# Seven-product down projection of one layer: where the weight combinations are formed, how the products are summed, and which engine norms the rows

## The reference

```python
def conv_ffn(h, rows, cols, w_up, w_dw, b_dw, w_down):
    up = h @ w_up                                   # 1024 -> 2 * 2816
    a, g = jnp.split(up, 2, axis=-1)
    ...                                             # 3x3 depthwise conv of g on the 16 x 64 grid
    g = g4.reshape(B, L, D_FF) + b_dw
    return (jax.nn.gelu(g) * a) @ w_down            # 2816 -> 1024

    ...
    x = layer_norm(ALPHA * x + g2[:, None, :] * ffn, p['ln2_g'], p['ln2_b'])
```

## Time and profile before

| | |
|---|---|
| runs | 1420.64, 1414.67, 1416.58 us; median 1416.58 |
| profiled execution | 1413.91 us, of which the span 1412.2 us |
| mean granted clock | 0.963 |
| PE busy | 1285.5 us (91%), 7739 matmuls |
| DVE busy | 1043.7 us (74%) |
| POOL busy | 636.2 us (45%) |
| ACT busy | 593.4 us (42%) |

### The profile page before, as it was taken

How to read it: one execution, slowest core, us unless ns; L and a number is a source line. 1 busy time by engine, 2 the same in 40 slices (tenths; PEclk the granted TensorE clock), 3 DMA queues, 4 the chain that set the end, 5 groups by cost and what they waited for, 6 DMA issues and landing times.

```text
span 1412.2 us, 21496 instructions
## 1 busy us (share of the span) xinstructions
PE 1285.5 (91%) x7739; PEld 1182.6 (84%) x7739; DVE 1043.7 (74%) x1563; ACT 593.4 (42%) x1018; POOL 636.2 (45%) x453
## 2 busy tenths in 40 slices
PE   5899999889998799988999999999999999999763
PEld 3689998788988677888999999999999878888642
DVE  7565669673566788879786777767656797887997
ACT  6533124435345734544344444444434543443321
POOL 1002998323343112349557666676656640001552
PEclk9899899999999899998999999999999999999886
DMA  9432231553425432202222231322312777654221
GB/s 345 130 88 83 64 90 45 172 174 75 110 75 194 164 113 98 75 16 69 72 92 93 69 108 55 107 87 74 97 51 67 260 268 244 209 192 172 90 74 60
DMA packets 145666, 166.69 MB, mean 118 GB/s; under 512 B 9303, under 2 KB 101939, under 8 KB 145331
## 3 DMA queue, kind: packets, MB, share of 16 engines
q1 hardware_dynamic: 145102, 160.88, 35.5%
q0 software_dynamic: 288, 4.72, 0.8%
q10 hardware_dynamic: 197, 0.06, 0.0%
HBM read 137.83 MB, written 27.80 MB: 117 GB/s over the span
## 4 chain that ended last, share of the span: by engine, by line
PE 70%; DVE 15%; issue 4%; ACT 4%; DMA 3%; POOL 3%; SPq 0%; DVEq 0%; ACTq 0%; POOLq 0%
PE ps L1149 12%; PE ps L1495 10%; PE ps L1493 10%; PE ps L1494 10%; PE ps L1525 4%; PE ps L1526 4%; PE ps L1527 4%; PE ps L1101 2%; DVE dwlo L3018 1%; DMA adaw<-in_w_ada 1%; PE ps L1060 1%; PE ps L1369 1%; PE ps L1371 1%; PE ps L1370 1%; DVE qk L2612 1%
## 5 line engine op out<-in xcount | busy, mean ns | idle before, releaser
L2924 DVE SCALAR_TENSOR_TENSOR ps<-gs,taps,ps 128x945 f32<-128x945 f32 (+2 forms) x176 | 215.8, 1226 | 36.2 <-ACT ps L1910 30.8
L1525 PE MATMUL ps<-dwhi,uhi 128*128 128x512 f32 x341 | 137.9, 404 | 26.5 <-DVE dwlo L3018 22.2
L1149 PE MATMUL ps<-h1hi,whi 128*128 128x384 f32 x432 | 155.1, 359 | 0.0
L1149 PE MATMUL ps<-h1lo,whi 128*128 128x384 f32 x432 | 147.6, 342 | 0.0
L1149 PE MATMUL ps<-h1hi,wlo 128*128 128x384 f32 x432 | 147.4, 341 | 0.0
L1526 PE MATMUL ps<-dwlo,uhi 128*128 128x512 f32 x341 | 136.3, 400 | 0.0
L1527 PE MATMUL ps<-dwhi,ulo 128*128 128x512 f32 x341 | 136.0, 399 | 0.0
L1525 PEld LDWEIGHTS ps<-dwhi,uhi 128*128 128x128 f32 x341 | 65.8, 193 | 46.3 <-issue 18.8
L2109 POOL TENSOR_TENSOR wlo<-raw,whi 128x512 fp32r<-128x512 f32 x46 | 68.9, 1500 | 71.9 <-ACT whi L1605 28.6
L1493 PE MATMUL ps<-thi,xhi 128*128 128x288 f32 x320 | 95.5, 299 | 3.0 <-issue 3.0
L1493 PE MATMUL ps<-thi,whi 128*128 128x288 f32 x320 | 94.2, 294 | 2.1 <-POOL wlo L2109 2.1
(11 more groups left out here) (422 smaller groups left out, 3891.6 us busy)
## 6 DMA issues: line engine op xcount, KB each, us to landing
raw<-in_w_up SPq DMA_DIRECT2D x78, 256.0 KB, 3.4
u_rows<-ub SPq DMA_DIRECT2D x22, 576.0 KB, 2.9
adaw<-in_w_ada SPq DMA_DIRECT2D x24, 512.0 KB, 3.9
raw<-in_w_in SPq DMA_DIRECT2D x40, 256.0 KB, 4.1
w_raw<-in_w_down SPq DMA_DIRECT2D x33, 256.0 KB, 5.1
adaw<-in_w_ada SPq DMA_DIRECT2D x8, 1024.0 KB, 10.6
u_raw<-u_rows SPq DMA_DIRECT2D x22, 320.0 KB, 5.9
raw<-u_rows SPq DMA_DIRECT2D x25, 256.0 KB, 5.3
```

Source lines behind the costliest of these rows:

```text
L1149: last = mm(ps[:, bank, 0:GN], a[:, n % 2, k * P:(k + 1) * P], b[:, kk, grp(g)], start=(kk == 0 and a is whi and b is h1hi), stop=(kk == K ...
L1525: mm(out, u_hi, w_hi, start=start, stop=False)
L2924: step(stt(a3[:, ro, co], g3[:, ri, ci], taps[:, tap:tap + 1], a3[:, ro, co], ALU.mult, ALU.add), 2 + m)
```

## The change

- **Weight combinations in the up projection.** The `t1` to `t4` of the down projection are gone. A new helper `t_parts` on DVE forms all four combinations of one step from the four blocks of w_down in a buffer `st`, with a wait between them, in the up projection: behind `ada3` in every second tile of the first four bodies (8 times) and in the first three tiles of the last body. SP loads `st` (two loads of 512 KB) and stores it to a new array `t_rows` in memory (1 MB) each time. In the down projection every product's weights are loaded through the ring `w_raw`.
- **`ub` is gone.** Its place holds `st`; u is written in place over `val` and stored from there, so ACT's copy of product 1 into `val` also waits for that store.
- **Order and chaining.** The products run D_U1, D_U2, D_S2, D_S1, D_S4, D_S3, D_U4, with a fixed set of banks each (SET). D_S2 is summed on top of D_U1 in PSUM (two of its tiles are written back to PSUM by ACT, `seed`), D_S4 on top of D_S1, D_S3 on top of D_U1 + D_S2, and D_U4 on top of that. ACT copies the intermediate sums out between products (`copy_u2`, `copy_at_end`).
- **Context rows** are done in D_U1 and D_U2 with six matmuls a step each, and no more in D_S4. Their weights' low parts in D_U2 (`xw_lo`) are POOL's, 11 instructions.
- **Norm.** `part` on DVE does gate, residual and statistics of half a row tile, `spread` the aggregate, `gain` normalises and applies gain and bias with two 128x1024 scalar_tensor_tensor. POOL only forms the nine 1/sqrt; ACT does nothing of the norm.
- **SP's order** is new in the down projection: the gate and norm rows (2 MB) are loaded behind D_U2's loads, the x rows of five tiles within D_S2, the others within D_U4, the first store within D_S4.

```diff
             def up_loads(b, jj, blk=None):
 ...
+                if blk is None:
+                    store_st(2 * b + jj, F_0 + 2 * b + jj + 1)
+                    if jj < 2:
+                        sp.wait_ge(st_out, SI_0 + 16 * (2 * b + jj + 1))
+                        load_st(2 * b + jj + 1)
+                elif jj % 2 == 0:
+                    store_st(2 * b + jj // 2, 2 * b + (F_0 + jj // 2 + 1))
+                else:
+                    sp.wait_ge(st_out, 32 * b + (SI_0 + 16 * (jj // 2 + 1)))
+                    load_st(2 * b + (jj // 2 + 1))
 ...
                 act.wait_ge(u_ready, j + (N_PLAIN + jj - 1))
+                act.wait_ge(u_out[par], 8 * j + (UO_0 + 16 * (1 + jj // 2)))
                 fn(halves(val[:, par, second]), ps[:, PC:PC + 2, 0:TC], ACT.Copy).then_inc(x5_copied, 1)
 ...
+            def t_parts(b, n):
+
+                def step(ins, m):
+                    ins.then_inc(st_step, 1)
+                    dve.wait_ge(st_step, 6 * b + (SS_0 + 3 * n + m))
+
+                w11, w12, w21, w22 = [st[:, q, :] for q in range(4)]
+                dve.wait_ge(st_in, 64 * b + (SI_0 + 32 * (n + 1)))
+                step(tt(w11, w12, w11, ALU.subtract), 1)
+                step(tt(w12, w22, w12, ALU.subtract), 2)
+                step(tt(w22, w22, w11, ALU.subtract), 3)
+                tt(w21, w21, w22, ALU.subtract).then_inc(t_formed, 1)
 ...
                 conv(j + (N_PLAIN + jj - 1), 1 - par)
                 if blk is not None:
                     ada3(b, jj, blk)
+                if blk is not None and jj % 2 == 0:
+                    t_parts(b, jj // 2)
+                if blk is None and jj < 3:
+                    t_parts(b, jj)
                 dve.wait_ge(pe_unit, s_unit(b, jj, 4) + 1)
 ...
+            def part(i, half):
+                t, slot, cols = TILE_OF[i], (2 * NT + i) % 4, slice(half * UC, (half + 1) * UC)
+                out, gate = z[t][:, cols], grows2[:, who(t), cols]
 ...
+                else:
+                    dve.wait_ge(pe_zt, N_ZT + 8 + i - 4)
+                    link(tt(out, ps[:, BANKS[0][t], :], gate, ALU.mult))
 ...
+                ins = stt(out, zt[(i - 1) % 4 if i else 4][:, cols], ALPHA, out, ALU.mult, ALU.add)
 ...
+                link(v.bn_stats(stats[:, slot, 6 * half:6 * half + 6], out))
 ...
+            def gain(i, halves=1):
 ...
+                    link(stt(out, out, mv[:, slot, 0:1], lnrows2[:, 0, cols], ALU.subtract, ALU.mult))
+                    stt(out, out, rstd[:, slot, :], lnrows2[:, 1, cols], ALU.mult, ALU.add
+                        ).then_inc(z_ready if halves == 1 else zl_ready, 1)
 ...
             for j in range(KF):
                 both_lo(D_S3, j)
                 if 3 <= j < 7:
                     c12(j - 3)
+                if j == 3:
+                    part(1, 1)
+                    spread(1)
                 if j == 4:
+                    part(2, 1)
+                    spread(2)
                 if j == 5:
+                    gain(1)
                 if j == 6:
+                    part(3, 1)
+                    spread(3)
                 if j == 7:
+                    gain(2)
                 if j == 8:
+                    part(4, 1)
+                    spread(4)
                 if j == 9:
+                    gain(3)
             for j in range(KF):
                 both_lo(D_U4, j)
                 if j == 0:
+                    gain(4)
                 if 3 <= j < 7:
+                    c22(j - 3)
+                if 4 <= j < 8:
+                    part(1 + j, 1)
+            part(5, 0)
+            spread(5)
+            part(6, 0)
+            spread(6)
+            gain(5)
+            part(7, 0)
+            spread(7)
+            gain(6)
+            part(8, 0)
+            spread(8)
+            gain(7)
+            gain(8, halves=2)
```

More of the change, by code:

```diff
@@ L499, in layer @@
         BANKS = ((0, 1, 4, 5), (2, 3, 6, 7))
-        D_U1, D_U2, D_S1, D_S2, D_S4, D_S3, D_U4 = range(7)
+        D_U1, D_U2, D_S2, D_S1, D_S4, D_S3, D_U4 = range(7)
+        SET = (0, 1, 0, 1, 1, 0, 0)
         TILE_OF = (LT, 4, 5, 6, 7, 0, 1, 2, 3)
+        T_ROW = {D_S1: 0, D_S3: 1, D_U4: 2, D_S2: 3}
         def s_count(name, j):
-            return F_0 + KF * ("S3", "S1", "S2", "S4").index(name) + j + 1
-        def t_count(name, j):
-            return F_0 + KF * ("T1", "T2", "T4", "T3").index(name) + j + 1
+            return F_0 + {"S3 ahead": j, "S1": KF + 2 * j, "S2": KF + 2 * j + 1, "S4": 3 * KF + j, "S3": 4 * KF + j}[name] + 1
         def ulo_count(m):
@@ L521, in u_index, with v_index, d_index @@
         def u_index(p, j):
-            return KF * {D_U1: 0, D_U2: 1, D_S2: 2, D_S4: 3, D_U4: 4}[p] + j
-        def w_index(p, j):
-            return KF * {D_U1: 0, D_U2: 1, D_S4: 2, D_U4: 3}[p] + (j - 4 if p == D_U4 else j)
+            return KF * {D_U1: 0, D_U2: 1, D_U4: 2}[p] + j
         def x_index(p, j):
-            return KF * {D_U1: 0, D_U2: 1, D_S1: 2, D_S2: 3, D_U4: 4}[p] + (j - 8 if p == D_U4 else j)
-        def d_index(kind, j):
-            return KF * ("u3", "w22", "w22 again").index(kind) + j
+            return KF * {D_U1: 0, D_U2: 1}[p] + j
+        def v_index(p, j):
+            return KF * {D_U2: 0, D_S2: 1, D_S4: 2}[p] + j
+        def d_index(p, j):
+            return KF * {D_U1: 0, D_S4: 1}[p] + j
         def u_landed(p, j):
@@ L859, in load_u @@
-                if p == D_S4:
-                    load_rows(dst[:, UC:UX], KF + j, slice(LAT, T), done)
-                elif p in (D_U1, D_U2):
+                    at((s_formed, s_count("S3 ahead", j + KF - ARING)) if j < ARING else ulo_count(KF * D_U2 + j - ARING))
+                else:
+                    at(ulo_count(KF * D_U2 + j + KF - ARING if j < ARING else KF * D_U4 + j - ARING))
+                if p == D_U4:
+                    load_rows(dst[:, 0:UC], KF + j, slice(0, UC), done)
+                else:
@@ L967, in _ @@
                 sp.wait_ge(u_out[par], UO_0 + 16 * (FT // 2))
+            for b in range(4):
+                sp.wait_ge(y_out[b], 16 * times(b))
             for j in range(KF):
@@ L971, in _ @@
                 load_x(D_U2, j)
[L972 to L989 removed]
+                load_v(D_U2, j)
+            sp.wait_ge(st_out, SI_0 + 16 * KF)
             sp.wait_ge(gate_out, 16)
@@ L1573, in _ @@
             for p in range(7):
-                ctx = p in (D_U1, D_U2, D_S4)
-                order = {D_U2: (2, 3, 0, 1), D_S1: (1, 2, 3, 0), D_S3: (1, 2, 3, 0)}.get(p, (0, 1, 2, 3))
+                ctx = p in (D_U1, D_U2)
+                order = (2, 3, 0, 1) if p in (D_U2, D_S2) else (0, 1, 2, 3)
                 for j in range(KF - N_TAIL if p == D_U4 else KF):
@@ L1583, in _ @@
                         last = tile_mms(p, j, i)
+                        if p in (D_S1, D_S3) and j == KF - 1 and i < H - 1:
+                            last.then_inc(pe_zt, 1)
                     if ctx and j < KF - 1:
@@ L3061, in t3 @@
[L3061 to L3070 removed]
+                tt(su2[j][:, :], v_part(D_S2, j), su2[j][:, :], ALU.subtract).then_inc(s_formed, 1)
```

694 lines of the change are left out of this document (258 added, 436 removed).

## The result

The changed kernel takes 1395.34 us (median of 4 runs, 1393.13 to 1398.87) against 1416.6: a ratio of 0.9849, 95% interval 0.9819 to 0.9879. On the chip of the first experiments it was 0.9876 (0.9854 to 0.9898). The prediction was 1391, with a range of 1375 to 1408. Spans: 1392.8 us against 1412.2.

A forecast was written before the change was run, and what follows sets the result against it. DVE, often standing behind POOL, was taken to hold up PE at the down projection's end. +13.6 (up projection), -3.5 (D_U1), -34.2 (end) gave -24.1 us, span 1388.1, and 1391 us forecast, range 1375 to 1408.

The forecast's parts named there:

- What bounded it: Down projection: some 40 us of PE waiting or at lower clock, 20.7 us DVE tail; DVE largely stands behind POOL.
- D_S3, D_U4 and the tail: End of the down projection: the end comes 81.2 us after D_S4 instead of 115.4, 34.2 us less.
- The stages between at zero: D_U2, D_S2, D_S1, D_S4: DVE's work fits PE's pace, transfers cost zero, upper bound 5 us.
- D_U1: First down-projection product: fewer DVE combinations take 3.5 us off, between 0 and 5.2, giving 46.6 us.
- The up projection: Four combinations in DVE's 3.20 us gap, taking turns with POOL, make PE wait: 1.7 us a tile, 13.6 for eight.
- The rule of the Trainium skill: Shared SBUF port lock: a turn of 2.0 us instead of 1.69, up projection's price 19 us, forecast 5 us later.
- The sum: Whole kernel: +13.6 - 3.5 - 34.2 = -24.1 us, span 1388.1.
- A: Up projection: the combinations are free there, -37.7 us, about 1378; chance 0.17.
- B: Clock and DVE keep the end, D_U2 transfers cost: 4 + 5 + 3 us more, 19 instead of 13.6, about 1405; chance 0.17.
- C: Up projection: each combination loses two turns to POOL, 3.3 us each, +26 us, 1442; chance 0.08.

The follow-up runs named there:

- e5: The kernel before with only gate and bias of the last norm moved from POOL to DVE: 1408.54 us, ratio 0.9936 to before.
- e4: The changed kernel with sixteen extra POOL instructions of 128x1024 on unused memory during the last eight row tiles: 1426.12 us, ratio 1.0056 to before.
- e0: The changed kernel run again without any edit, as yardstick: 1399.05 us, ratio 0.9876 to before.
- e1: The split version: changed kernel with two combinations ahead of the add of product 4, two behind that of product 5: 1381.51 us, 0.9766 of before.
- e6: The changed kernel with all four combinations of a step behind the add of product 5: 1381.52 us, ratio 0.9757 to before.
- e7: The mixed version: changed kernel with all four combinations behind product 5's add in looped bodies, unchanged in the last body: 1380.73 us, 0.9748 of before.
- e2: The changed kernel with combinations on one column instead of 512, loads, stores and waits kept, results wrong: 1383.07 us, ratio 0.9764 to before.
- e3: e2 plus eleven 128x512 subtractions on DVE in D_U1, where the first weight combination stood before: 1387.19 us, ratio 0.9778 to before.

## Why the prediction was right, step by step

*What bounded it.* Right. The turns behind POOL are shown from both sides: taken away alone (e5) they give 8 to 9 us in spite of 20 us of added work, put back alone (e4) they cost 25 to 27. They are not all of it: most of the end's gain, 24.8 of 33.6 us, came with the lighter work of DVE, which the prediction had in its sum.

*D_S3, D_U4 and the tail*, forecast 81.2 us after D_S4: 81.9 to 82.0 in the later executions with the same end (e0, e1, e6, e7), 83.7 in the first, where PE's clock fell behind a wait of 2.3 us (0.63 and 0.51 from 1366 to 1370, 0.98 over the stretch). The forecast of PE's end, 66.8, was met at 66.7 to 66.8 in the later ones (68.5 in the first). The tail is 15.2 where 14.4 was forecast. DVE takes up the first finished tile 58.8 us after D_S4 (forecast 58.7), and its work from there is 20.7 us instead of 20.0: each pass of `gain` takes 1.28 us and not 1.21, and 0.75 and not 0.70 in halves, a form that the kernel before did not show.

*The stages between at zero.* Right: 134.6 us in every kernel, although the transfers in D_U2's 40.8 us came to 359 GB/s, where the prediction had 267 for the heaviest steps. ACT waited for the store of `val` once, 0.6 us.

*D_U1*, forecast 46.6: 46.8.

*The up projection* is the term that was mis-sized, 13.6 forecast and 17.1 measured (476.5 against 459.4). The turn was right (1.66 us an operation, the next one 1.70 behind it, against 1.69 in the earlier trace rows), and so was the wait in a paired tile: 1.3 us, and 1.55 with what follows it, for 1.7. The period of two tiles is 46.0 us, forecast 46.2, before 44.5. The seven such tiles cost 10.9 us. Wrong was to take eight tiles alike. In the first one DVE is behind to begin with: in the kernel before PE already waits there (3.3 us between two matmuls), so there is no gap of 3.20 us. The add of product 4 comes 7.2 us after the end of the convolution instead of 1.6, and the pause of PE is 7.4 us, since DVE happened to be 1.5 us further ahead of PE in this execution than in the one before the change; in e0, where it was behind, the pause is 10.5. In all this tile costs 4.6 us here and 6.8 in e0, and it is what varies most from one execution to the next. The last 1.6 us came in the fifth body, where the clock fell to 1.2 GHz for a moment around PE's small products: the period of that tile was 27.4 us against 25.8. With combinations of one column (e2) it is 27.4 as well, so it is not their work; why the clock fell there stays open.

The rule of the Trainium skill ("SBUF — State Buffer", "SBUF: two separate sides") taken to the letter, each turn as long as both instructions together (2.0 us), would have given 8.0 us for the four instead of the 6.8 measured. The trace agrees with the turns and not with their sum: POOL's instruction of 1.30 us and DVE's of 0.69 come at 1.70. And the turns end where DVE has no pause: one POOL instruction was held up over 12 and 17 of DVE's (9.29 and 12.07 us, e3).

*The sum*: -19.4 us in span where -24.1 was forecast, 4.7 less. The up projection is 3.5 of them, the end 2.4 (most of it the clock of that one execution), D_U1 0.1; the program up to the up projection was 1.3 us shorter than in the execution of before, which no term forecast.

The rivals: A (free) is what another place gives: the changed kernel paid 17.1 us, the split version 3.3, and its 1381.5 us lie 3.5 above A's 1378. Of B only the up projection's 19 came near; its 4, 5 and 3 us for the end, the clock and the transfers did not come, beyond 2.5 at the end of the first execution. Its own terms add up to 1408 and not to the 1405 that it states, the edge of the range. C did not come up: no combination took over 1.78 us, so none lost two turns.

The best complete version measured is the split one, 0.9766 and 0.9742 of the kernel before in two comparisons; the one with all combinations behind (0.9757) and the mixed one (0.9748) can't be told from it.

## What to carry to other kernels

When DVE and POOL both work on SBUF operands, price a new DVE operation by the turn (here 1.7 us) and not by its own time (0.7 us), and look at which of its gaps POOL is idle in; the same four operations cost some 15 us in one gap and 1 us spread over two. Look at POOL's side too: where DVE has no pause, it is POOL that may stand still. Ahead of a wait that PE sits behind, put only what fits; work with slack belongs behind the last thing another engine is waiting for. And before moving work out of a stage, see whether anybody waited in that stage: of the 44 moved combinations only the 11 of `t1` stood in and ahead of a product where PE lost time.

## What the runs showed of the hardware

- DVE and POOL on two SBUF operands each alternate at 1.70 us with POOL instructions of 128x512 (1.30 alone) and DVE ones of the same size (0.69 alone); beside a POOL instruction of 128x1024 a DVE pass of 1.28 us takes 3.3 to 3.4 us (e4).
- They don't always alternate: beside 12 and 17 such DVE instructions without a pause, none of them longer than alone, one POOL instruction of 128x512 took 9.29 us (before) and 12.07 (e3).
- Linking operations by a semaphore wait costs them no extra turn: linked they went at 1.70 us, as the unlinked ones of the earlier trace rows.
- PE accumulated in PSUM on top of sums that earlier products had left there, and on two tiles that ACT had written, at the same 0.227 us a matmul (134.6 us for 594).
